# Moving three weight loads, a bias table and three matrix products from the gather loop to behind its last gather

## The chip, the cores and the metric

The kernel runs on one core of one Trainium2 chip. The metric is device time in microseconds (us), the median of three runs. Everything is float32 (the feed-forward part works with products of split numbers).

## What is computed

Two transformer blocks over 256 tokens of 1024 features, batch 1. The change touches the seam between them: the last step of the first block (a layer that picks 128 experts for every token) and the first projections of the second block.

```python
def peer(h, w_pq, sub_keys, u_emb, v_emb):          # end of the first block
    ...                                             # 8 heads, top 16 of 128 x 128 keys each
    def chunk(args):
        hx, idx, g = args                           # idx: 128 experts of each of 128 tokens
        a = jax.nn.gelu(jnp.einsum("ced,cd->ce", u_emb[idx], hx), approximate=False)
        return jnp.einsum("ce,ced->cd", g * a, v_emb[idx])
...
x = x + peer(h2, ...); x = rmsnorm(x, final_g)
...
h = _rmsnorm(x, norm_mix[0])                        # start of the second block, layer 0
p = h @ ev_w_in[0]
qa, ka, va = three slices of p, 512 columns each
c_q, c_kv  = the next 768 and 256 columns of p      # called cqkv below: 1024 columns, two chunks
a_out = _dilated_mixture(qa, ka, va, t5_bias)       # attention with a bias table over distances
b_out = _mla(c_q, c_kv, ...)
```

## The kernel before, in words

The 256 tokens are two tiles of 128 (t = 0, 1), one token per partition. Each engine runs its own list of instructions in the order in which it is written, with semaphores between them.

**The gather loop.** For each tile there are 128 rows of experts (8 heads times 16, `SLOTS`), 256 in all. Row n is one indirect transfer (GpSimd, L568) that brings for each of the 128 tokens the 1024 numbers of u and the 1024 of v of one expert, 1 MB in all, into one of 8 buffers (`NROWS`, tile name `gath`, which the profile shows as `pool`). VectorE multiplies the u half with the token and sums it (L1566, `dot`), ScalarE makes the weight of the row, two rows at a time (L1143, L1147), and a diagonal matrix of it (L1153), TensorE multiplies the v half with the diagonal and adds it up in PSUM (L850). Then the buffer is spent (`row_spent`), and the gather of row n + 8 may be issued: `wait_spent` before L568. VectorE also selects the experts of later heads between its dots, and TensorE makes the scores for that (`query`, L611 and L825) in the first tile at every eighth row, up to row 39.

**Weights** come as one stream of chunks of up to 2 MB through a ring of three slots (`ring`), issued by SyncE at L532 in one fixed list, each when the last use of the chunk three before it is through. The chunks of this case are `va` (one) and `cqkv` (two), which follow the four chunks of the queries, `pq`; then `qa`, `ka`, `kpe_uq`. So `va` is loaded when the product `("pq", 3)` is done, and `cqkv` 0 and 1 after `("pq", 5)` and `("pq", 7)`, the last of which stands at rows 15 and 31 of tile 0.

**The bias table** `tab` (1.5 MB, `t_scratch` in the profile) is issued by GpSimd at L574, right after the gather of row 128, since its place is taken by the keys of the queries until then. VectorE waits for it before the attention `attA`.

**The second block in the shadow of the first.** When tile 0 is complete, its final norm and the next norm are made at rows 2 to 10 of the next tile, the transposes at row 15 (`NORM_SLOT`), and TensorE makes tile 0's products of `va`, `cqkv` 0 and `cqkv` 1 (`token_chunk`, 8 multiplications of 128x512 each, L611) at rows 31, 55 and 79 (`TOKEN_SLOTS`) of tile 1. ScalarE copies each out of PSUM (`token_copy`, L942) 8 rows later (`TOKEN_LAG`).

**Behind the last row**, the same is done for tile 1: VectorE adds the sums (L1576), ScalarE and VectorE make the two norms (L946, L947, L1334, L1341), VectorE clears `kaz` (L481, L482), TensorE transposes (L644), VectorE applies the gain (L1348), TensorE makes the three products of tile 1 (L611), then in split form the products `qa` and `ka` (L716 to L718), whose weights ScalarE and VectorE split into two parts (L1003, L1328), and then the attention `attA` begins (L674). PSUM has six banks for all of this, taken in turn in the order of one list, `fill_list`.

Of the kernel before, what the change touches and what calls it, by code (L numbers as in the profile page):

```python
# [22 lines left out]
P = 128  # L23
S = 256
NT = S // P
# [5 lines left out]
PH, TOPK, NKEYS = 8, 16, 128  # L31
SLOTS = PH * TOPK
# [3 lines left out]
HEADS2 = 8  # L36
# [90 lines left out]
EARLY_QUERIES = 7  # L127
TOKEN_CHUNKS = (("va", 0), ("cqkv", 0), ("cqkv", 1))
NORM_SLOT = 15
TOKEN_SLOTS = (31, 55, 79)  # L130
TOKEN_LAG = 8
QUERY_EVERY = 8


def fill_list():
    out = [("t5",)] + norm_fills("N1") + fm_fills("glu", 4) + tm_fills("q1", 2) + tm_fills("kv1")
    out += fm_fills("gate", 4)
    out += [("q1T", t, half) for t in range(NT) for half in range(2)] + [("k1T",), ("mean",), ("var",)]
    out += attention_fills("att1", QH)
    out += fm_fills("convout", 2) + fm_fills("attno", 2) + tm_fills("wout", 2)  # L140
    out += norm_fills("N2")
    out += QUERY_ORDER
    for t in range(NT):
        out += [("mix0", t, half) for half in range(2)] + [(name, i, t) for name, i in TOKEN_CHUNKS]
    out += fm_fills("qa") + fm_fills("ka")
    out += attention_fills("attA", HEADS2)
    out += norm_fills("cT") + tm_fills("kpe") + tm_fills("uqa") + tm_fills("uqb") + tm_fills("ukv", 2)
    out += [(n, t, half) for n in ("qmT", "kmT") for t in range(NT) for half in range(2)]
    out += attention_fills("attB", HEADS2) + tm_fills("evout", 2)
    for layer in range(2):  # L150
        if layer:
            out += norm_fills("mix1") + tm_fills("uz") + tm_fills("vz") + fm_fills("qd") + fm_fills("kd")
            out += tm_fills("vd") + [("gating", t) for t in range(NT)] + [("coutT", t) for t in range(NT)]
            out += attention_fills("attD", HEADS2) + tm_fills("odout", 2)
        out += norm_fills("ffn%d" % layer) + fm_fills("gu%d" % layer, KF // 2)
        out += [("down%d" % layer, half, t) for half in range(2) for t in range(NT)]
    return out
# [47 lines left out]
def last_use(chunk):  # L205
    return LAST_USE.get(chunk, (chunk[0], chunk[1], 1))
# [10 lines left out]
def build(nc, stream, consts, t5const, params, rows, keys_in, late_rows, x_in, positions, t5_in, rpb_in, uv, out):  # L217
    with ExitStack() as ctx:
# [300 lines left out]
        @block.sync  # L519
        def _(sp):  # L520
            sp.dma_start(x[:, :, :], x_in.rearrange("(t p) d -> p t d", p=P)).then_inc(x_landed, 16)
            sp.dma_start(cst[:, :], consts).then_inc(const_landed, 16)
            sp.dma_start(par[:, :], params).then_inc(param_landed, 16)
            for n, (name, width) in enumerate(CHUNKS):
                if n >= NSLOT:
                    before = CHUNKS[n - NSLOT][0]
                    if before in CHUNK_SPLIT:
                        sp.wait_ge(lo_split, CHUNK_SPLIT[before])
                    else:
                        sp.wait_ge(bank_filled, FILL_NO[last_use(before)] + 1)  # L530
                src = stream[CHUNK_AT[n]:CHUNK_AT[n + 1]].rearrange("(p w) -> p w", p=P)
                sp.dma_start(ring[:, n % NSLOT, 0:width], src).then_inc(chunk_landed[n % NSLOT], 16)  # L532
            for t in range(NT):
                sp.wait_ge(out_ready, t + 1)
                sp.dma_start(out[P * t:P * t + P, :], xn[:, t, :]).then_inc(out_stored, 16)
            sp.wait_ge(out_stored, 16 * NT)


        @block.gpsimd
        def _(gp):  # L540
            gp.dma_start(pos_i[:, :], positions).then_inc(pos_landed, 16)
            gp.dma_start(t5hot, t5const[0:32, :]).then_inc(t5_landed, 16)
            gp.dma_start(t5ln, t5const[32:32 + HEADS2, :]).then_inc(t5_landed, 16)
            gp.dma_start(t5tab, t5_in).then_inc(t5_landed, 16)
            gp.dma_start(row[:, :], rows.to_broadcast([P, NROW])).then_inc(row_landed, 16)
            gp.dma_start(keys.rearrange("p m n -> p (m n)"), keys_in).then_inc(keys_landed, 16)

            nc.gpsimd.memset(rpb_pad, 0.0).then_inc(rpb_cleared, 1)
            gp.wait_ge(rpb_cleared, 1)
            rp = rpb_pad.rearrange("h (r c) -> h r c", r=15)  # L550
            gp.dma_start(rp[:, :, 48:79], rpb_in).then_inc(rpb_landed, 16)
            gp.wait_ge(rpb_landed, 16)
            for r in range(RPB_ROWS):
                gp.dma_start(rpb_dram[:, r], rp[:, r + 4, :].unsqueeze(1).to_broadcast([HEADS2, GRID, P])
                             ).then_inc(rpb_stored, 16)

            wait_emptied(gp, ("t5",))
            gp.dma_start(t5_dram, t5vec.unsqueeze(1).to_broadcast([HEADS2, P, REL])).then_inc(t5_stored, 16)
            gp.wait_ge(t5_stored, 16)
            gp.wait_ge(rpb_stored, 16 * RPB_ROWS)  # L560


            for n in range(NT * SLOTS):
                if n % TOPK == 0:
                    gp.wait_ge(selected, n // TOPK + 1)
                if n >= NROWS:
                    wait_spent(gp, n - NROWS)
                gp.indirect_dma_start(out=gath[:, n % NROWS, :], out_offset=None, in_=uv,  # L568
                                      in_offset=bass.IndirectOffsetOnAxis(ap=experts[:, n:n + 1], axis=0)
                                      ).then_inc(row_landed_in[n % NROWS], 16)  # L570
                if n == SLOTS:

                    gp.wait_ge(bank_filled, FILL_NO[("sc", PH - 1)] + 1)
                    gp.dma_start(tab[:, :, :], bass.AP(tensor=t5_dram.tensor, offset=S - P,  # L574
                                                       ap=[[REL - 1, P], [P * REL, HEADS2], [1, TABW]])
                                 ).then_inc(taba_landed, 16)


            gp.wait_ge(bank_filled, FILL_NO[("attA", "OT", 0, 0)] + 1)
            for qr in range(2):  # L580
                for h in range(HEADS2):

                    gp.dma_start(tab[GRID * qr:GRID * qr + GRID, h, :].rearrange("p (r c) -> p r c", r=6),
                                 bass.AP(tensor=rpb_dram.tensor, offset=(h * RPB_ROWS + 1 - qr) * GRID * P + GRID - 1,
                                         ap=[[P - 1, GRID], [GRID * P, 6], [1, GRID]])).then_inc(tabd_landed, 16)
            gp.dma_start(row[:, LATE["final2"][0]:LATE["final2"][1]],
                         late_rows[:, 0:D].to_broadcast([P, D])).then_inc(late_landed, 16)
            gp.dma_start(row[:, LATE["v_gain"][0]:LATE["v_gain"][1]],
                         late_rows[:, D:D + CW].to_broadcast([P, CW])).then_inc(late_landed, 16)
            gp.wait_ge(tabd_landed, 16 * 2 * HEADS2)  # L590
            blocks = tab[:, :, :].rearrange("p h (r c) -> p (h r) c", c=GRID)
            nc.gpsimd.tensor_tensor(blocks, blocks, c_("namask").unsqueeze(1).to_broadcast([P, 6 * HEADS2, GRID]),
                                    ALU.add).then_inc(tabd_ready, 1)
# [3 lines left out]
        def _(pe):  # L597
# [234 lines left out]
            for t in range(NT):  # L832
                if t:
                    pe.wait_ge(sums_added, 2 * t)
                for k in range(SLOTS):
# [4 lines left out]
                        queries += 2  # L840
                    if t and k == NORM_SLOT:
                        tile_transposes("mix0", 0, xn[:, 0, :])
                    if t and k in TOKEN_SLOTS:
                        if k == TOKEN_SLOTS[0]:
                            wait_tile("mix0", 0)
                        name, i = TOKEN_CHUNKS[TOKEN_SLOTS.index(k)]
                        token_chunk(name, i, 0)
                    pe.wait_ge(diag_ready, n + 1)
                    for half in range(2):
                        last = nc.tensor.matmul(psum[:, RB + half, :], diag[:, n % NDIAG, :],  # L850
# [4 lines left out]
                    if k < SLOTS - 1:  # L855
                        last.then_inc(row_spent, 1)

            tile_transposes("mix0", 1, xn[:, 1, :])
            wait_tile("mix0", 1)
            for name, i in TOKEN_CHUNKS:  # L860
                token_chunk(name, i, 1)
            pe.wait_ge(h_split, 4)
            for q in range(FIRST_PART[0], GU):
                split_feature_major(0, q, (m_hi, m_lo))
# [65 lines left out]
        def _(act):  # L930
# [206 lines left out]
            for pair in range(NT * SLOTS // 2):  # L1137
# [26 lines left out]
                if unit == PH and k == 4:  # L1164
                    act.wait_ge(x_normed, 1)
                    root(x[:, 0, :], xn[:, 0, :], ssq[:, 0:1], 0, D)
                slot = 2 * (pair - SLOTS // 2) + 1 - TOKEN_LAG
                if slot in TOKEN_SLOTS:
                    token_copy(TOKEN_SLOTS.index(slot), 0)

            act.wait_ge(sums_added, 2 * NT)
            root(x[:, 1, :], xn[:, 1, :], ssq[:, 1:2], 1, D)
            act.wait_ge(x_normed, NT)
            root(x[:, 1, :], xn[:, 1, :], ssq[:, 1:2], 1, D)
            token_copy(0, 1)
            split_high(0, 6)
            token_copy(1, 1)
            split_high(0, 7)
            token_copy(2, 1)
            for t in range(NT):  # L1180
# [621 lines left out]
```

## Time and profile before

| | |
|---|---|
| median of 3 runs | 1775.72 us (1775.6 to 1777.1) |
| the profiled execution | 1774.15 us |
| its span, first to last instruction | 1772.1 us |
| granted TensorE clock, mean | 0.953 |
| gathers, first issued to last landed | about 359 to 1036 us |
| TensorE busy | 1515.9 us (86%) |
| VectorE, ScalarE, GpSimd busy | 959.1, 561.8, 315.6 us |
| bytes moved by DMA | 428.67 MB, mean 242 GB/s |
| gathers (queue q0, nearly all) | 279.20 MB |
| weights (queue q1) | 148.33 MB |

How to read it: the busy shares are averages over stages with different limits. TensorE leads in sum, but in the 677 us of gathers the DMA engines are the busiest resource, and on both sides of them TensorE is. What an instruction costs is therefore read from its own stage: from the chain of waits there, and from the DMA rate beside it.

### The profile page before, as it was taken

Reading aid. Unit: us, or ns where it says so; the run is one execution under the profiler, and the core shown is the slowest. Engines: PE = TensorE matmul, PEld = TensorE weight load, DVE = VectorE, ACT = ScalarE, POOL = GpSimd, SP = SyncE. Lnnn points to the kernel's source line nnn. Section 1 sums busy time; section 2 is a strip of 40 time slices with the busy share of each in tenths; the row PEclk is TensorE's granted clock in tenths of the full one; section 3 lists DMA queues with packets and bytes.
Section 4 is the critical chain, followed back from the end, with each engine's and each line's share of the span. In section 5 each row is a group of like instructions: output and inputs, shape, how many; then the busy total and the mean of one; then the engine's idle time right before and its main releaser. Section 6 shows DMA issues by size and latency. Waiting matters only on the chain.

```text
span 1772.1 us, 18024 instructions
## 1 busy us (share of the span) xinstructions
PE 1515.9 (86%) x6822; PEld 1057.0 (60%) x6822; DVE 959.1 (54%) x1916; ACT 561.8 (32%) x1195; POOL 315.6 (18%) x296
## 2 busy tenths in 40 slices
PE   6999699879987777678988769986999969869997
PEld 5768587555533322233333227664999869559996
DVE  2896431375576677677766443233555454245554
ACT  1001530123333333433333224342333334333333
POOL 2000000033344444344445400400000000000000
PEclk9999899989999999899999989998999979989999
DMA  9964013299999999999999935313344523124551
GB/s 258 201 199 171 4 48 143 95 387 385 395 420 419 420 419 418 394 419 410 410 419 415 420 141 223 102 48 142 146 187 190 194 102 147 68 108 180 190 190 48
DMA packets 52022, 428.67 MB, mean 242 GB/s; under 512 B 6880, under 2 KB 7032, under 8 KB 9824
## 3 DMA queue, kind: packets, MB, share of 16 engines
q0 software_dynamic: 40720, 279.20, 40.8%
q1 hardware_dynamic: 11216, 148.33, 22.0%
q8 instruction: 54, 0.88, 0.2%
q14 instruction: 32, 0.26, 0.0%
HBM read 422.50 MB, written 4.98 MB: 241 GB/s over the span
## 4 chain that ended last, share of the span: by engine, by line
PE 66%; DMA 17%; DVE 9%; ACT 5%; issue 2%; POOL 1%; DVEq 0%; SPq 0%; ACTq 0%; POOLq 0%
PE psum L611 24%; DMA pool<-uv,experts 16%; PE psum L850 11%; PE psum L716 9%; PE psum L717 9%; PE psum L718 9%; DVE pool L1566 2%; PE psum L644 2%; PE psum L674 2%; DMA ring<-stream 1%; DVE w_lo L1328 1%; ACT xn L946 1%; ACT diag L1153 1%; POOL pool L568 1%; ACT L1143 1%
## 5 line engine op out<-in xcount | busy, mean ns | idle before, releaser
L850 PE MATMUL psum<-pool,diag 128*128 128x512 f32 x1024 | 487.7, 627 | 132.0 <-ACT diag L1153 122.0
L850 PEld LDWEIGHTS psum<-pool,diag 128*128 128x128 f32 x1024 | 196.1, 199 | 418.1 <-issue 210.9
L1566 DVE CUSTOM_DVE_ANT_0 pool<-pool,xn 128x1024 f32<-128x1024 f32 x256 | 313.8, 1226 | 207.5 <-DMA pool<-uv,experts 205.9
L568 POOL DMA_INDIRECT pool<-uv,experts x256 | 283.7, 1108 | 703.9 <-PE psum L850 359.0
L1328 DVE TENSOR_TENSOR w_lo<-ring,w_hi 128x2048 fp32r<-128x2048 f32 x76 | 173.9, 2292 | 182.7 <-ACT w_hi L1003 182.7
L1003 ACT ACTIVATE w_hi<-ring 128x2048 fp32r<-128x2048 f32 x76 | 145.0, 1911 | 284.7 <-PE psum L718 284.7
L716 PE MATMUL psum<-h_hi,w_hi 128*128 128x256 f32 x704 | 201.4, 286 | 22.4 <-DVE h_lo L1367 22.4
L717 PE MATMUL psum<-h_lo,w_hi 128*128 128x256 f32 x704 | 201.0, 286 | 0.0
L718 PE MATMUL psum<-h_hi,w_lo 128*128 128x256 f32 x704 | 200.9, 285 | 0.0
L611 PE MATMUL psum<-hT,ring 128*128 128x256 f32 x768 | 171.1, 385 | 5.5 <-DMA ring<-stream 2.9
L611 PEld LDWEIGHTS psum<-hT,ring 128*128 128x128 f32 x768 | 148.1, 193 | 28.8 <-issue 5.1
L716 PEld LDWEIGHTS psum<-h_hi,w_hi 128*128 128x128 f32 x704 | 137.1, 195 | 22.8 <-issue 22.8
L717 PEld LDWEIGHTS psum<-h_lo,w_hi 128*128 128x128 f32 x704 | 137.2, 195 | 0.0
L718 PEld LDWEIGHTS psum<-h_hi,w_lo 128*128 128x128 f32 x704 | 137.0, 195 | 0.0
L1143 ACT ACTIVATE acts<-dots 128x2 f32<-128x2 f32 x128 | 25.9, 202 | 333.9 <-DVE dots L1566 333.8
L611 PE MATMUL psum<-ring,hT 128*128 128x512 f32 (+2 forms) x288 | 111.5, 547 | 6.4 <-DVE hT L1502 3.2
L1439 DVE SCALAR_TENSOR_TENSOR pool<-pool,par 128x256 f32<-128x256 f32 x236 | 93.8, 489 | 0.0
L1153 ACT ACTIVATE diag<-cst,coef 128x128 f32<-128x128 f32 x256 | 89.7, 394 | 12.2 <-PE psum L850 8.1
L611 PEld LDWEIGHTS psum<-ring,hT 128*128 128x128 f32 x288 | 53.6, 195 | 62.9 <-issue 56.2
L942 ACT ACTIVATE att<-psum 128x512 f32<-128x512 f32 x69 | 40.5, 588 | 92.4 <-PE psum L611 69.4
L716 PE MATMUL psum<-w_hi,gu_hi 128*128 128x512 f32 x176 | 68.5, 389 | 0.0
L717 PE MATMUL psum<-w_lo,gu_hi 128*128 128x512 f32 x176 | 68.5, 389 | 0.0
(234 smaller groups left out, 1774.3 us busy)
## 6 DMA issues: line engine op xcount, KB each, us to landing
ring<-stream SPq DMA_DIRECT2D x66, 2048.0 KB, 7.9
pool<-uv,experts POOLq DMA_INDIRECT x256, 12.5
ring<-stream SPq DMA_DIRECT2D x3, 1024.0 KB, 6.0
t_scratch<-att POOLq DMA_DIRECT2D x1, 2048.0 KB, 90.8
rpb_scratch<-att POOLq DMA_DIRECT2D x7, 256.0 KB, 28.2
ring<-stream SPq DMA_DIRECT2D x1, 1792.0 KB, 10.2
row<-rows POOLq DMA_DIRECT2D x1, 1672.0 KB, 15.4
ring<-stream SPq DMA_DIRECT2D x1, 1664.0 KB, 7.0
```

The source lines that it names most:

```text
L568: gp.indirect_dma_start(out=gath[:, n % NROWS, :], out_offset=None, in_=uv, in_offset=bass.IndirectOffsetOnAxis(ap=experts[:, n:n + 1], ax ...
L611: last = nc.tensor.matmul(dst, lhsT, rhs, start=(i == 0), stop=(i == len(pairs) - 1))
L716: nc.tensor.matmul(dst, lhsT[0], rhs[0], start=start, stop=False)
L717: nc.tensor.matmul(dst, lhsT[0], rhs[1], start=False, stop=False)
L718: return nc.tensor.matmul(dst, lhsT[1], rhs[0], start=False, stop=stop)
L850: last = nc.tensor.matmul(psum[:, RB + half, :], diag[:, n % NDIAG, :], gath[:, n % NROWS, D + 512 * half:D + 512 * half + 512], start=k = ...
L1003: nc.scalar.activation(part_split(split_tensors(layer, q)[0], layer, q), part_raw(layer, q), ACT.Copy).then_inc(hi_split, 1)
L1143: nc.scalar.activation(acts[:, b, :], dots[:, b, :], ACT.Gelu).then_inc(acts_ready, 1)
L1153: nc.scalar.activation(diag[:, n % NDIAG, :], ident, ACT.Copy, scale=coef[:, b, j:j + 1]).then_inc(diag_ready, 1)
L1328: V.tensor_tensor(lo, part_raw(layer, q), hi.bitcast(F32), ALU.subtract).then_inc(lo_split, 1)
L1439: n = mark(V.scalar_tensor_tensor(y[:, m, :], src, tap, y[:, m, :], ALU.mult, ALU.add))
L1566: ins = V.tensor_tensor_reduce(out=row_u, in0=row_u, in1=xn[:, n // SLOTS, :], scale=1.0, scalar=0.0, op0=ALU.mult, op1=ALU.add, accum_out ...
```

## The change

- SyncE waits before the chunk `va` until row 247 of 256 is spent. That is what the last gather waits for too, so `va` and, right behind it, `cqkv` 0 and 1 are issued together with the last gather.
- GpSimd issues `tab` behind the last gather instead of behind that of row 128.
- TensorE no longer makes tile 0's three products at rows 31, 55 and 79. Behind the last row it makes `va` of tile 0, the transposes of tile 1, `va` of tile 1, and then `cqkv` 0 of both tiles and `cqkv` 1 of both.
- ScalarE's copies of tile 0's products move behind the norms of tile 1, between the others.
- The list of PSUM banks follows the new order.

```diff
@@ fill_list
-    for t in range(NT):
-        out += [("mix0", t, half) for half in range(2)] + [(name, i, t) for name, i in TOKEN_CHUNKS]
+    out += [("mix0", 0, 0), ("mix0", 0, 1), ("va", 0, 0), ("mix0", 1, 0), ("mix0", 1, 1), ("va", 0, 1)]
+    out += [("cqkv", i, t) for i in range(2) for t in range(NT)]
@@ SyncE, before the load of a chunk
+                if (name, width) == (("va", 0), 4096):
+                    wait_spent(sp, NT * SLOTS - NROWS - 1)
                 src = stream[CHUNK_AT[n]:CHUNK_AT[n + 1]].rearrange("(p w) -> p w", p=P)
@@ GpSimd
-                if n == SLOTS:
-
-                    gp.wait_ge(bank_filled, FILL_NO[("sc", PH - 1)] + 1)
-                    gp.dma_start(tab[:, :, :], bass.AP(...)).then_inc(taba_landed, 16)
+            gp.wait_ge(bank_filled, FILL_NO[("mix0", 0, 0)] + 1)
+            gp.dma_start(tab[:, :, :], bass.AP(...)).then_inc(taba_landed, 16)
@@ TensorE
-                    if t and k in TOKEN_SLOTS:
-                        if k == TOKEN_SLOTS[0]:
-                            wait_tile("mix0", 0)
-                        name, i = TOKEN_CHUNKS[TOKEN_SLOTS.index(k)]
-                        token_chunk(name, i, 0)
...
+            wait_tile("mix0", 0)
+            token_chunk("va", 0, 0)
             tile_transposes("mix0", 1, xn[:, 1, :])
             wait_tile("mix0", 1)
-            for name, i in TOKEN_CHUNKS:
-                token_chunk(name, i, 1)
+            token_chunk("va", 0, 1)
+            for i in range(2):
+                for t in range(NT):
+                    token_chunk("cqkv", i, t)
@@ ScalarE
-                slot = 2 * (pair - SLOTS // 2) + 1 - TOKEN_LAG
-                if slot in TOKEN_SLOTS:
-                    token_copy(TOKEN_SLOTS.index(slot), 0)
...
+            token_copy(0, 0)
             token_copy(0, 1)
+            token_copy(1, 0)
             split_high(0, 6)
             token_copy(1, 1)
+            token_copy(2, 0)
             split_high(0, 7)
             token_copy(2, 1)
```

TensorE's order from the second tile on, before. L850 are the products of the rows (two for each row), L644 the transposes of `mix0`, L611 with `ring,hT` the products of `va` and `cqkv`, eight each:

```order
81 L850 MATMUL psum<-pool,diag 128x512 x208
82 L644 MATMUL psum<-cst,xn 128x128 x8
83 L850 MATMUL psum<-pool,diag 128x512 x32
84 L611 MATMUL psum<-ring,hT 128x512 x8
85 L850 MATMUL psum<-pool,diag 128x512 x48
86 L611 MATMUL psum<-ring,hT 128x512 x8
87 L850 MATMUL psum<-pool,diag 128x512 x48
88 L611 MATMUL psum<-ring,hT 128x512 x8
89 L850 MATMUL psum<-pool,diag 128x512 x98
90 L644 MATMUL psum<-cst,xn 128x128 x8
91 L611 MATMUL psum<-ring,hT 128x512 x24
```

and with the change, where L850, L644 and L611 have become L843, L642 and L609:

```order
81 L843 MATMUL psum<-pool,diag 128x512 x208
82 L642 MATMUL psum<-cst,xn 128x128 x8
83 L843 MATMUL psum<-pool,diag 128x512 x226
84 L609 MATMUL psum<-ring,hT 128x512 x8
85 L642 MATMUL psum<-cst,xn 128x128 x8
86 L609 MATMUL psum<-ring,hT 128x512 x40
```

The 24 products that stood between the rows are gone from there; 8 of them stand ahead of the last transposes and 16 among the 40 behind.

SyncE's queue with the change; the rows ahead of the new wait are the chunks up to the last of `pq`:

```order
6 L532 DMA ring<-stream 128x2048 [waits bank_filled]
7 L532 DMA ring<-stream 128x4096 [waits bank_filled] x14
8 L532 DMA ring<-stream 128x4096 [waits row_spent,bank_filled]
9 L532 DMA ring<-stream 128x4096 [waits bank_filled] x4
10 L532 DMA ring<-stream 128x3328 [waits bank_filled]
```

Row 8 there is `va`, which waits for the rows of the gather loop too; behind it stand `cqkv` 0 and 1, `qa` and `ka`, which keep their own waits.

## Rows read from the trace of the kernel before

**Rows 1.** The page, 40 slices of 44.3 us: rate that the DMA moved.

```profile
GB/s 258 201 199 171 4 48 143 95 387 385 395 420 419 420 419 418 394 419 410 410 419 415 420 141 223 102 48 142 146 187 190 194 102 147 68 108 180 190 190 48
```

**Rows 2.** Chain of waits, early gathers: start us, us, what.

```profile
380.19 14.55 PE psum L850 x28
...
477.28 13.80 PE psum L850 x28
...
496.73 11.47 DMA pool<-uv,experts
```

**Rows 3.** Stretches, early gathers: us, PE, PEld, DVE, ACT, POOL busy, PEclk, DMA share, GB/s.

```profile
476.00:480.00 4.00, 2.72 (x3) 1.17 (x4) 2.92 (x11) 3.28 (x14) 0.00 (x0) 0.62 0.98 414
480.00:484.00 4.00, 4.00 (x10) 1.86 (x9) 0.63 (x2) 0.80 (x2) 1.87 (x2) 0.95 0.94 344
484.00:488.00 4.00, 4.00 (x11) 1.80 (x10) 2.17 (x7) 1.38 (x5) 1.88 (x2) 1.00 0.97 330
```

**Rows 4.** DMA queues 475 to 481 us; chunk issued 471.75 us, size, us to landing.

```profile
q1 hardware_dynamic: 125, 2.02, 79.2%
q0 software_dynamic: 80, 0.52, 20.9%
...
ring<-stream SPq DMA_DIRECT2D x1, 2048.0 KB, 12.1
```

**Rows 5.** Chain of waits at the switch to tile 1.

```profile
702.36 16.66 DMA pool<-uv,experts
...
755.11 12.60 DMA pool<-uv,experts
```

**Rows 6.** Who waited for whom, whole run: us in total, times, longest.

```profile
PE psum L850 <- DVE x L1576: 9.8, 1, 9.8
```

**Rows 7.** Stretches in tile 1; the first, third, fourth hold one product each.

```profile
796.00:812.00 16.00, 15.90 (x37) 7.14 (x38) 12.86 (x38) 7.37 (x20) 5.31 (x5) 1.00 0.98 393
812.00:856.00 44.00, 36.41 (x76) 14.75 (x74) 31.31 (x80) 14.52 (x46) 22.21 (x19) 0.92 1.01 421
856.00:872.00 16.00, 15.51 (x37) 6.76 (x36) 9.93 (x21) 5.13 (x19) 5.38 (x6) 1.00 0.99 398
...
917.00:933.00 16.00, 15.19 (x36) 6.82 (x37) 12.18 (x36) 8.02 (x22) 5.91 (x6) 1.00 1.00 403
```

**Rows 8.** Last gather: its issue, us to landing, queue 1022 to 1036 us, its dot.

```profile
1022.51 0.94 POOL L568 DMA_INDIRECT pool<-uv,experts  x1 [0.78 <-PE psum L850]
...
pool<-uv,experts POOLq DMA_INDIRECT x1, 13.5
...
q0 software_dynamic: 691, 4.98, 85.7%
...
1036.00 1.23 DVE L1566 CUSTOM_DVE_ANT_0 pool<-pool,xn 128x1024 f32<-128x1024 f32 x1 [1.13 <-DMA pool<-uv,experts]
```

**Rows 9.** Timeline behind the last row: start us, us, instruction, [idle before it, releaser].

```profile
1049.75 1.97 PE L644 MATMUL psum<-cst,xn 128*128 128x128 f32 x8 [7.58 <-DVE xn L1341]
...
1051.96 1.29 DVE L1348 TENSOR_TENSOR hT<-psum,par 128x512 f32<-128x512 f32 x2
...
1053.35 22.76 PE L611 MATMUL psum<-ring,hT 128*128 128x512 f32 x48 [1.63 <-DVE hT L1348]
```

**Rows 10.** Chain of waits: one product of tile 0 (16 records).

```profile
798.09 6.87 PE psum L611 x16
```

**Rows 11.** Stretches behind the gathers.

```profile
1052.00:1054.00 2.00, 0.65 (x1) 0.50 (x2) 1.97 (x4) 0.00 (x0) 0.00 (x0) 0.50 0.00 0
...
1058.00:1060.00 2.00, 2.00 (x6) 0.87 (x5) 0.00 (x0) 0.00 (x0) 0.00 (x0) 1.00 0.00 0
...
1076.00:1099.00 23.00, 23.00 (x193) 22.93 (x191) 7.93 (x11) 10.22 (x19) 0.00 (x0) 1.00 0.64 249
```

**Rows 12.** Timeline: split of qa's weights; first use of the bias table.

```profile
1070.59 1.91 ACT L1003 ACTIVATE mw_hi<-ring 128x2048 fp32r<-128x2048 f32 x1 [7.59 <-DMA ring<-stream]
...
1101.88 0.76 DVE L1298 SCALAR_TENSOR_TENSOR att<-psum,tab 128x256 f32<-128x256 f32 x2 [7.55 <-PE psum L674]
```

More of the change, by code:

```diff
@@ L129 @@
 NORM_SLOT = 15
-TOKEN_SLOTS = (31, 55, 79)
-TOKEN_LAG = 8
 QUERY_EVERY = 8
@@ L570, in _ @@
                                       ).then_inc(row_landed_in[n % NROWS], 16)
-                if n == SLOTS:
-                    gp.wait_ge(bank_filled, FILL_NO[("sc", PH - 1)] + 1)
-                    gp.dma_start(tab[:, :, :], bass.AP(tensor=t5_dram.tensor, offset=S - P,
-                                                       ap=[[REL - 1, P], [P * REL, HEADS2], [1, TABW]])
-                                 ).then_inc(taba_landed, 16)
+            gp.wait_ge(bank_filled, FILL_NO[("mix0", 0, 0)] + 1)
+            gp.dma_start(tab[:, :, :], bass.AP(tensor=t5_dram.tensor, offset=S - P,
+                                               ap=[[REL - 1, P], [P * REL, HEADS2], [1, TABW]])
+                         ).then_inc(taba_landed, 16)
             gp.wait_ge(bank_filled, FILL_NO[("attA", "OT", 0, 0)] + 1)
```

## The prediction, made before the changed kernel ran

> **What bounds the kernel now.** I read the page's slices first, then the chain of waits, then the DMA rate in short stretches, and the timeline behind the gathers last. From the ninth slice to the 23rd the DMA moves 385 to 420 GB/s [rows 1], and 420 is what it reaches at best there. So the gathers are close to a stage that is bound by bytes, and a first sum would say: 6.29 MB of weights (three chunks of 2048 KB) and 1.57 MB of table (1536 KB) leave it, which at 420 GB/s is 15.0 and 3.7 us. The chain of waits says that this is only partly so. From 380 to 496 us it is TensorE, whose rows and query products follow each other (28 records of row products in 14.55 us, and so on), with no gather in it [rows 2]; the first piece in it that is a gather begins at 496.73. All three chunks are loaded before that (the last is issued at 471.75 [rows 4]). From 497 us to the last gather the chain runs through gathers, one after the other. Behind the last row first the norms and then TensorE are the bound: it computes without a gap from 1053.35 to 1099 us [rows 9, 11].
>
> **The chunks, where they leave.** A chunk hurts the gathers if the DMA would have been busy with them at that time. The last of the three, issued at 471.75 us, is the clearest [rows 4]: while it runs the DMA is full (414 GB/s), but in the 8 us right behind it the rate falls to 344 and 330 [rows 3]. A DMA that slackens there has caught up: nearly all gathers that may be issued have landed, and the next waits for TensorE to spend a row. TensorE is busy throughout those 8 us. So the chunk filled time that TensorE's pace left free. The other two are loaded earlier in the same stretch of the chain, where TensorE's pieces are whole [rows 2]. I take the gain as 0. The other bound is the whole 15.0 us of their bytes; a loss isn't to be had from taking a load away. I stay at 0 since the slack rows lie exactly behind the chunk.
>
> **The table, where it leaves.** It is issued at the switch to tile 1, in the stretch that the gathers do bound. The gather behind it stands 16.66 us in the chain, the next such piece 12.60 [rows 5]: 4.1 us, and the bytes alone make 3.7. What follows is the addition of tile 0's sums, for which TensorE waits 9.8 us [rows 6], so all of it can come out. Gain 4.1 us, bounds 3.0 and 4.1. At its new place it lands behind the last gather, by my sum near 1057 us of the old clock even with all that is below; the first to read it is VectorE at 1101.88 [rows 12], 45 us of cover.
>
> **The products of tile 0, where they leave.** Each takes TensorE 6.87 us in the middle of the rows [rows 10]. Their stretches of 16 us move 393, 398 and 403 GB/s, where a stretch of 44 us between them moves 421 [rows 7]. Against 420 that is 27, 22 and 17 GB/s for 16 us each, 1.06 MB or 2.5 us. The rest of their 20.6 us is hidden by transfers today. Gain 2.5 us, bounds 0 and 4. ScalarE's three copies leave too, beside an engine that waits for the dots; I put them at nothing.
>
> **The chunks, where they arrive.** This is the first of two costs. SyncE now waits for the row that the last gather waits for too, so all three chunks go out with it. What queues behind that wait on SyncE is only `cqkv` and `qa`, and `qa` waits for a product behind the gathers anyway. But at that moment some gathers are still under way: the last is issued at 1022.51, takes 13.5 us to land, and 4.98 MB move in between [rows 8]. The question is who is served first. The row to ask is the time in which chunk and gathers ran together, 475 to 481 us: q1, the weights, moved 2.02 MB, q0, the gathers, 0.52 [rows 4]. At 79% of the 423 GB/s that both make up three chunks take 18.7 us, while the gathers move 1.7 MB; the last gather lands when all is through, (4.98 + 6.29) MB / 420 = 26.8 us instead of 11.9. So the end of the gathers is late by the full 6.29 MB, 15.0 us, and TensorE, which makes the last sum 6 us after that, has nothing to do meanwhile: `va` of tile 0, though landed, stands behind the last row in its order. Cost 15.0 us. The lower bound is a fair share by bytes: as much weight as gather until the last gather is in, 4.98 / 0.42 = 11.9 us. Gathers first would be 0, which the row speaks against by four to one.
>
> The Trainium skill ("DMA: Bandwidth & Descriptors", section "Queues, rings and completion order") says that each DMA engine goes round robin between the queues it has work for, a packet at a time. Taken as equal bytes for both it would give the 11.9 us and not 15.0; the trace's 2.02 against 0.52 MB doesn't agree with that reading.
>
> **The products, where they arrive.** The second cost. `va` of tile 0 comes first and falls into the 7.58 us in which TensorE waits for the norm [rows 9]: 6.87 us fit, and VectorE's clearing of `kaz` holds the next step to 1051.96 in any case. If it fits worse, by a cold clock, up to 2 us. Behind the transposes stand 5 products instead of 3. The three take 22.76 us, of which the first records run at a granted clock of 0.50 and the later ones at 1.00 [rows 9, 11]. With TensorE at work in the gap I expect the full clock from the start: 5 x 6.87 = 34.4 us, so +11.6; with the same slow start it would be +13.7. All of it is on the path, since TensorE is without a gap until the attention. ScalarE and VectorE keep up: `qa` is still loaded after `va` of tile 1, 8 us later it is split [rows 12], long before TensorE comes to it, and `ka` is loaded two products before its turn. The banks repeat after six, and the first reuse (`cqkv` 1 of tile 0 over `va` of tile 0) is five products later.
>
> **The sum**, against the profiled execution: -0 - 4.1 - 2.5 + 15.0 + 11.6 = +20.0 us, 1774.15 to 1794.2. The median of the runs is 1.6 above that execution, so 1795.7.
>
> **Rivals.**
> - *A fair share.* Chunks and gathers move equal bytes: 11.9 for 15.0, 1792.6. For it: two queues on the same engines. Against it: [rows 4]. 0.14.
> - *The bytes counted after all.* Without the chunks the early gathers run ahead and hand on some of the 15.0 us: half of it gives 1788.2, all of it 1780.7. For it: 385 to 395 GB/s in slices that are nearly full [rows 1]. Against it: the chain. 0.10.
> - *Gathers first.* The indirect transfers, being queued already, are served and the chunks fill what is left: no 15.0 us, and 1780.7. `va` would land 5 us behind the last gather, still before its product. 0.05.
> - *Faster.* The weights leave a byte-bound stage (-15.0) and, served last, come back for nothing: -15.0 - 4.1 - 2.5 + 11.6 = -10.0, 1765.7. It turns when gain less delay of the chunks passes 5.0 us, as 11.6 of products stand against 6.6 of the rest. It needs both of the two above. 0.03.
> - *A cold clock.* With one gather in about 12 us for some 19 us TensorE idles, and the last two pairs of rows and the first product run at half clock, as at 1052 us [rows 11]: 3.7 us for a pair turns into 7.4, and `va` outlasts its gap. Up to 6 us more, 1801.7. Against it: the clock is back at 1.00 within 4 to 6 us of work there [rows 11]. 0.13.
> - *The change isn't what it says*: some wait keeps the chunks back until behind the last row. Then no 15.0 us, but TensorE waits some 10 us for `va`, near 1790. I find none. 0.02.
>
> **How the numbers follow.** The forecast as such has 0.52, the cases beside it 0.14, 0.10, 0.05, 0.03, 0.13 and 0.02. The range 1783 to 1802 takes in the fair share, half or less of the bytes, and most of the cold clock, with 0.85 of the chance by these cases. A measurement of this kernel can't tell 0.2% (3.6 us) from no change. Faster by more than that: 0.03. Within: 0.02, where the faster case gets only part of its gain. Slower: 0.95.
>
> **What would show it.** In the profile of the changed kernel: the last gather issued near 1016 us, 6.6 earlier, and 28 us or so to its landing instead of 13.5; in between q1 with four times the bytes of q0; the last dot near 1044. The rate near 480 us still below 420 with no weights in it, which would confirm the 0; if the chain of waits reaches its first gather well before 496 and the last gather is issued before 1013, the 0 was wrong. Rates near 420 through rows 31, 55 and 79 of tile 1. `va` of tile 0 within the norms, then 80 records of products in 34 to 36 us, and the attention's first scores near 1120 instead of 1100. I would be wrong above all if the last gather takes less than 20 us to land.

## The result, and the profile after

| | before | changed |
|---|---|---|
| median | 1775.66 us (1769.5 to 1777.1, 4 runs) | 1801.3 us (1799.4 to 1801.8, 4 runs) |
| profiled execution | 1774.15 | 1801.6 |
| its span | 1772.1 | 1799.5 |
| mean granted clock | 0.953 | 0.955 |

The ratio is 1.0149, 95% interval 1.0124 to 1.0174. The kernel is slower by 25.6 us where +20.0 was forecast. One execution among those of the experiments below (of the products alone) took 6936 us, and is left out of every ratio.

The chain of waits of the changed kernel (start us, us, what; the lines have moved by two to seven, so L843 is the old L850, L609 the old L611, L1563 the old L1566), from the loop's last rows on:

```profile
997.75 13.48 DMA pool<-uv,experts
...
1013.73 3.71 PE psum L843 x8
...
1017.70 28.20 DMA pool<-uv,experts
...
1045.93 1.23 DVE pool L1563
...
1048.40 6.38 PE psum L843 x8
...
1065.93 34.57 PE psum L609 x80
...
1125.07 1.11 PE psum L672 x4
...
1151.89 29.43 PE psum L609 x92
```

The gather in the chain before the last takes 13.48 us, the last one 28.20, where [rows 8] have 13.5. The pair of rows behind it takes 6.38 us and not 3.71. Then come 80 records of products in 34.57 us, for 48 in 22.76 [rows 9]. The DMA queues between 1019.5 and 1038 us (packets, MB, share of 16 engines) tell who moved. Here q1 carries the weights and q0 the gathers:

```profile
q1 hardware_dynamic: 336, 4.98, 63.5%
q0 software_dynamic: 407, 2.90, 37.5%
```

The stretches of that time show what TensorE had of it (us, PE, PEld, DVE, ACT, POOL busy, granted clock, DMA share, GB/s):

```profile
1028.00:1032.00 4.00, 0.00 (x0) 0.00 (x0) 1.23 (x2) 0.00 (x0) 0.00 (x0) 0.74 1.05 444
1032.00:1036.00 4.00, 0.00 (x0) 0.00 (x0) 0.01 (x1) 0.00 (x0) 0.00 (x0) 0.50 1.03 433
1036.00:1040.00 4.00, 1.54 (x2) 0.84 (x3) 1.23 (x2) 1.38 (x5) 0.00 (x0) 0.50 0.98 407
1040.00:1044.00 4.00, 4.00 (x6) 1.52 (x5) 0.45 (x1) 0.00 (x0) 0.00 (x0) 0.56 0.97 382
```

The DMA is full and every engine waits for it; the clock stands at 0.50 when rows come again.

Against the spans of both profiled executions the account is as follows. Each time is a start in a timeline or chain of waits of either kernel.

| stretch | before | changed | difference | forecast |
|---|---|---|---|---|
| start to the last gather's issue | 1022.51 | 1017.70 | -4.8 | -6.6 |
| issue to the last dot | 13.49 | 28.23 | +14.7 | +15.0 |
| last dot to attA's first scores | 64.67 | 79.14 | +14.5 | +11.6 |
| first scores to the end of the span | 671.4 | 674.4 | +3.0 | 0 |
| sum | | | +27.4 | +20.0 |

In the third line are 11.8 us of products and 2.7 us of the last pair of rows. The fourth line holds no work that the change touches.

### The profile page after: what moved, and what is told of

Its sections match the earlier page's. It is cut to its first block, busy times and chain, and to the rows that moved or that the text cites. A ratio compares the mean times of both kernels' runs of the same rounds, so it can differ in the third digit from the quotient of the medians.

```text
span 1799.5 us, 18025 instructions
## 1 busy us (share of the span) xinstructions
PE 1518.7 (84%) x6822; PEld 1056.7 (59%) x6822; DVE 958.6 (53%) x1916; ACT 561.8 (31%) x1195; POOL 308.1 (17%) x296
## 4 chain that ended last, share of the span: by engine, by line
PE 62%; DMA 20%; DVE 10%; ACT 5%; issue 3%; POOL 0%; DVEq 0%; SPq 0%; ACTq 0%; POOLq 0%
PE psum L609 23%; DMA pool<-uv,experts 19%; PE psum L843 10%; PE psum L714 8%; PE psum L715 8%; PE psum L716 8%; DVE pool L1563 3%; PE psum L642 2%; PE psum L672 2%; DMA ring<-stream 1%; DVE w_lo L1325 1%; ACT diag L1150 1%; ACT xn L943 1%; ACT L1140 1%; ACT att L968 1%
## 5 line engine op out<-in xcount | busy, mean ns | idle before, releaser
L843 PE MATMUL psum<-pool,diag 128*128 128x512 f32 x1024 | 490.7, 628 | 161.6 <-ACT diag L1150 156.0
L843 PEld LDWEIGHTS psum<-pool,diag 128*128 128x128 f32 x1024 | 194.9, 199 | 452.5 <-ACT diag L1150 239.5
L1563 DVE CUSTOM_DVE_ANT_0 pool<-pool,xn 128x1024 f32<-128x1024 f32 x256 | 313.4, 1226 | 218.3 <-DMA pool<-uv,experts 214.4
L568 POOL DMA_INDIRECT pool<-uv,experts x256 | 276.3, 1079 | 707.3 <-PE psum L843 367.0
L609 PE MATMUL psum<-hT,ring 128*128 128x256 f32 x768 | 171.2, 385 | 5.5 <-DMA ring<-stream 2.9
L609 PEld LDWEIGHTS psum<-hT,ring 128*128 128x128 f32 x768 | 148.1, 193 | 28.8 <-issue 5.1
L609 PE MATMUL psum<-ring,hT 128*128 128x512 f32 (+2 forms) x288 | 110.3, 545 | 8.0 <-DVE hT L1499 3.2
L609 PEld LDWEIGHTS psum<-ring,hT 128*128 128x128 f32 x288 | 54.5, 202 | 62.6 <-issue 54.0
## 6 DMA issues: line engine op xcount, KB each, us to landing
rpb_scratch<-att POOLq DMA_DIRECT2D x7, 256.0 KB, 28.2
```

Of the source, the lines that this page charges most:

```text
L609: last = nc.tensor.matmul(dst, lhsT, rhs, start=(i == 0), stop=(i == len(pairs) - 1))
L1563: ins = V.tensor_tensor_reduce(out=row_u, in0=row_u, in1=xn[:, n // SLOTS, :], scale=1.0, scalar=0.0, op0=ALU.mult, op1=ALU.add, accum_out ...
```

## The experiments

### The early loads of the chunks: what were they worth?

The changed kernel alone says much. In the stretches around the place where the last chunk used to be loaded, it has no weights to move:

```profile
476.00:480.00 4.00, 2.72 (x3) 1.17 (x4) 3.86 (x11) 3.29 (x14) 0.00 (x0) 0.62 0.81 274
480.00:484.00 4.00, 4.00 (x10) 1.85 (x9) 1.71 (x6) 0.96 (x3) 2.17 (x2) 0.96 0.38 84
484.00:488.00 4.00, 4.00 (x11) 1.80 (x10) 1.88 (x5) 1.33 (x5) 2.49 (x3) 1.00 1.02 416
```

Where the kernel before moved 414, 344 and 330 GB/s [rows 3], this one moves 274, 84 and 416: for some 4 us it has next to nothing to do, and TensorE's busy time is the same. The first gather in the chain starts at 496.72 us, as before at 496.73 [rows 2]. To take nothing else away, the kernel before ran with these loads cut down to 32 of 4096 columns, so that the products compute with what stands in the ring:

```diff
+                if name in TOKEN_CHUNKS:
+                    src, width = src[:, 0:32], 32
                 sp.dma_start(ring[:, n % NSLOT, 0:width], src).then_inc(chunk_landed[n % NSLOT], 16)
```

> The kernel before, with the early loads of the three chunks cut to 32 of 4096 columns, so 6.2 MB less are moved; the products of va and cqkv use what stands in the ring, and the result is not the reference's. My theory (the early loads lie in time that TensorE's pace leaves free): 0, at most -1 us. Rival (bytes bound the whole gather loop): -15 us, 1761.

Measured: 1777.42 us against 1777.1, ratio 1.0004 (0.9991 to 1.0017). So with 6.2 MB less nothing is gained in the time, or 1.6 us at most by the interval. Its chain of waits has the same pieces:

```profile
375.39 14.57 PE psum L852 x28
...
472.50 13.81 PE psum L852 x28
...
491.95 10.70 DMA pool<-uv,experts
```

It runs 4.8 us ahead of the kernel before, but its first gather was issued that much earlier already (354.46 against 359.26 us): from the first to the 49th gather both take 137.5 us. From there to the last gather's issue it is 524.8 us against 525.8, so up to 1 us of gain may hide in the scatter.

### The table alone

```diff
-                if n == SLOTS:
-                    gp.wait_ge(bank_filled, FILL_NO[("sc", PH - 1)] + 1)
-                    gp.dma_start(tab[:, :, :], ...)
+            gp.wait_ge(bank_filled, FILL_NO[("mix0", 0, 0)] + 1)
+            gp.dma_start(tab[:, :, :], ...)
```

> Only the bias table moves behind the last gather; weights and products stay where they were. My theory: 4.1 us of the gathers' time come out at the switch to tile 1 and nothing is paid, so -4 to -5 us against the kernel before, about 1771. Rival (the next wait takes it up, since the buffers are full there anyway): within 1 us of before.

Measured: 1772.78 against 1777.1 us, ratio 0.9973 (0.9962 to 0.9984). A second measurement:

> The table alone behind the last gather, in more rounds, beside the version with the moved third product. My theory: ratio 0.996 to 0.998.

Measured: 1773.77 against 1776.46, ratio 0.999 (0.9981 to 1.000), 2.7 us by the medians and 1.8 by the ratio, which is less than was expected. The first gave 4.3 and 4.8. From the 49th gather's issue to the last it takes 522.6 and 522.9 us in the two profiles, against 525.8 before. I take the gain as 3.0 us, at the lower bound of the forecast's term and not the 4.1 taken; the executions alone leave room for 0 to 7 us.

### Products and table, but the chunks early

This is the changed kernel without these two lines:

```diff
-                if (name, width) == (("va", 0), 4096):
-                    wait_spent(sp, NT * SLOTS - NROWS - 1)
```

> The change without SyncE's new wait: the chunks are loaded early as before, table and products of tile 0 stand behind the gathers. My theory: +11.6 for the products, -4.8 for what the loop gains (as the changed kernel's last gather shows), so about +7, 1783; the last gather lands 13.5 us after its issue and not 28. Rival (the weights' early loads did cost the gathers something): the early loads come back, the last gather is issued later than in the changed kernel by up to 15 us, and this kernel is as slow as it, 1800.

Measured: 1785.39 against 1777.1 us, ratio 1.0038 (1.0025 to 1.0051). The chain of waits has both halves of the theory, the last gather at its old length and the 80 records:

```profile
1019.44 13.55 DMA pool<-uv,experts
...
1035.48 3.71 PE psum L841 x8
...
1050.36 36.13 PE psum L607 x80
```

The rival is out as to its size: with the early loads back the last gather isn't issued 15 us later but 1.7 (1019.44 against 1017.70), or 1.9 counted from the 49th gather (522.9 us against 521.0). The loads are all that differs up to there, so these 1.9 us are what the early loads cost, if they aren't scatter. The wait that SyncE got costs 15.9 us by the medians (1801.3 and 1785.4) and 19.7 by the ratios, so it costs far more than it buys.

### The products alone

> Only the products of tile 0 (and ScalarE's copies) move behind the gathers; chunks and table are loaded as before. My theory: +11.6 to +13.4 behind the gathers (five products where three were), -1 in the loop, so +11 to +12 against before. Rival (the products did cost the loop the 2.5 us or more of the forecast): +9 or less.

Measured: 1791.8 us against 1776.24 (1792.1 with the execution of 6936 us), ratio 1.0091 (1.0074 to 1.0108), above what was expected. The profile was of that execution and can't be used. A second measurement:

> The kernel in which only the products of tile 0 move, once more, since its first profile was of a disturbed execution. Its times lay 15.9 us above before (1792.1), where with the table moved too the same edit cost 12.6 (1785.4 against 1772.8 with the table alone). My theory: about 13.4 behind the gathers, and the rest is the scatter of a few us between executions, so +12 to +14 now. Rival (the table at its old place costs more when the products are gone from the loop, or the loop is slower without them): +16 again, and the last gather is issued 2 us or more later, counted from the first gather, than the 663.3 of before.

Measured: 1789.53 against 1776.46, +13.1, ratio 1.0076 (1.0057 to 1.0095). The products behind take 36.27 us (+13.5), and from the 49th to the last gather it is 525.3 us against 525.8. The loop got 0.4 us out of losing three products of 6.87 us each. The table at its old place doesn't cost more when they are gone: +13.1 lies within what was expected, and from the first to the last gather's issue it is 662.8 us, where 663.3 and 2 more would have spoken for that rival.

### The chunks after the last gather

The changed kernel, with another wait for the first chunk:

```diff
                 if (name, width) == (("va", 0), 4096):
-                    wait_spent(sp, NT * SLOTS - NROWS - 1)
+                    sp.wait_ge(row_landed_in[NROWS - 1], 16 * NT * SLOTS // NROWS)
```

> The changed kernel, but SyncE waits until the last gather has landed before it loads the three chunks. My theory (chunks and gathers share the DMA and the gathers lose): the last gather is back to 13.5 us, the last row is through 15 us earlier, the last pair of rows runs at the full clock (-2.7), and the first chunk is there about 8 us after the last landing, so its product still lies mostly in the gap before the norm: 15 to 18 us faster than the changed kernel, 1784 to 1786. Rival (the loss comes from TensorE's products alone and the DMA would have waited in any order): no more than 5 us faster than the changed kernel.

Measured: 1783.25 us against 1777.1, ratio 1.0034 (1.0023 to 1.0044), 18 us less than the changed kernel. Its timeline and chain:

```profile
1017.10 13.55 DMA pool<-uv,experts
1030.72 8.92 DMA ring<-stream
1039.89 8.65 PE psum L609 x16
...
1050.41 34.57 PE psum L609 x80
```

Only 13.6 us later do the same bytes start, the gather is back at 13.55 us, and TensorE waits 3 us for the first chunk. To load the weights *later* brings the last landing 15 us forward. This is the plainest proof that the delay of the last gather comes from what ran beside it.

### One chunk beside the last gathers, not three

```diff
                 if (name, width) == (("va", 0), 4096):
                     wait_spent(sp, NT * SLOTS - NROWS - 1)
+                if (name, width) == (("cqkv", 0), 4096):
+                    sp.wait_ge(row_landed_in[NROWS - 1], 16 * NT * SLOTS // NROWS)
```

> The changed kernel, but only the chunk va goes out with the last gather; cqkv 0 and 1 wait until that gather has landed. My theory (each chunk beside the last gathers delays them by its full bytes, 5.0 us): the last gather takes 18.5 us from issue to landing, and the time is 4 to 5 us above that of the kernel in which all three wait (1783 on the chip of that run), 10 to 11 above before. Rival (a fair share by bytes): one chunk ends before the last gather either way, so the landing can't tell it, but the queue's bytes in the first 6 us do: two of weights for two of gathers, against 2.0 to 0.5 by my theory.

Measured: 1787.53 against 1776.24 us, ratio 1.0063 (1.0046 to 1.008); 0.29% or 5 us above the kernel in which all three wait (1.0034), each against the kernel before that ran beside it. The last gather and its dot, in the timeline:

```profile
1018.17 0.94 POOL L570 DMA_INDIRECT pool<-uv,experts  x1 [0.78 <-PE psum L845]
...
1036.61 1.23 DVE L1565 CUSTOM_DVE_ANT_0 pool<-pool,xn 128x1024 f32<-128x1024 f32 x1 [1.17 <-DMA pool<-uv,experts]
```

From issue to dot it is 18.4 us. The chain of waits goes another way here, through a gather two before it (issued at 1013.18, 18.37 us), as each of the last four gathers is held up alike (17.6 or 18.4 us to landing). So 13.5, 18.4 and 28.2 us for none, one and three chunks: 4.9 us for each, close to 2.1 MB at 420 GB/s.

The shares of the two queues can be read where both have work. First this kernel, 1021 to 1027 us, then the changed one, 1021 to 1042 us, which is all the time that its three chunks move:

```profile
q1 hardware_dynamic: 108, 1.77, 69.8%
q0 software_dynamic: 120, 0.85, 33.9%
...
q1 hardware_dynamic: 412, 6.21, 70.1%
q0 software_dynamic: 406, 2.67, 30.5%
```

That is 2.1 and 2.3 to one, neither the one to one of the rival nor the four to one of the forecast and the expectation. In packets it is 108 to 120 and 412 to 406: both queues get through nearly as many packets, and a packet of weights is more than twice as large (15.1 KB against 6.6 in the changed kernel). The four to one came from [rows 4], and there the queue of the gathers had little to move. In the kernel before GpSimd waited for spent buffers:

```profile
474.60 0.94 POOL L568 DMA_INDIRECT pool<-uv,experts  x1 [8.18 <-PE psum L850]
481.05 0.93 POOL L568 DMA_INDIRECT pool<-uv,experts  x1 [5.52 <-PE psum L850]
```

Only one gather was issued between 466 and 481 us, and from 476 to 479 us q0 moved 0.14 MB beside 1.10 of q1. At two to one, too, the chunks are through before the last gather (1042 against 1046 us), and so their full bytes count.

### The changed kernel once more

> The changed kernel once more, beside the others on one chip. My theory: ratio to before 1.013 to 1.016 as in its first measurement, and in a second profile the same 28 us from issue to landing of the last gather and over 5.5 us for the last pair of rows; of the 3.0 us that its first profile lost behind the first scores of attA, part or all is chance of the clock and changes. Rival (that loss belongs to the change): it stays at 3 us, attA's first scores to the end taking 674 us again against 671.4 before.

Measured: 1800.49 against 1776.24 us, ratio 1.0131 (1.0109 to 1.0153). Its chain repeats the two marks:

```profile
1015.94 28.19 DMA pool<-uv,experts
...
1046.62 6.32 PE psum L843 x8
```

The last pair takes 6.3 to 6.4 us in both profiles of this kernel, and 3.70 or 3.71 us in those of all kernels here whose last gather takes 13.5 us. So the 2.7 us go with the idle time before it: TensorE stands idle for 11.06 us, makes the pair before the last in 6.2 us, is idle for 3.72 and makes the last one in 6.4, at a granted clock of 0.50 (1036 to 1040 and 1048 to 1051 us). The loss behind attA's first scores came again too, against what was expected: 674.5 us from there to the end, and the 92 records of products behind that attention took 29.43 us. But that stretch has three lengths, whatever the kernel: 26.15 us in the kernel before, in both profiles of the table alone, with one chunk and in one of the two profiles of the version below, 27.76 with the late chunks, and 29.4 to 29.5 in the changed kernel (twice), the products alone, products with table, the other profile of the version below, and the kernel with the cut loads, which differs in nothing there from the one before. What differs is how long the clock stands at 0.50 within it: the kernel before had 4 us at 0.57, the changed one, whose three rows follow, about three times as long:

```profile
1132.00:1136.00 4.00, 4.00 (x8) 1.70 (x8) 0.00 (x0) 0.20 (x1) 4.00 (x8) 0.57 0.65 152
...
1152.00:1156.00 4.00, 4.00 (x24) 4.00 (x24) 0.00 (x0) 0.20 (x1) 4.00 (x7) 0.60 0.62 152
1156.00:1160.00 4.00, 4.00 (x13) 2.97 (x14) 0.00 (x0) 0.20 (x1) 3.86 (x7) 0.50 0.62 151
1160.00:1164.00 4.00, 4.00 (x7) 1.52 (x7) 0.00 (x0) 0.00 (x0) 2.89 (x1) 0.62 0.59 200
```

It isn't a matter of the work in that stretch. Of the six profiles of kernels with all of tile 0's products behind the gathers four have 29.4 us, of the six others two; that the change makes it likelier can't be excluded and was not settled. But the whole way from the first scores to the end scatters more than that: 674.7 and 669.3 us in the two profiles of the table alone, 675.3 with the cut loads, 671.4 in the one profile of the kernel before, 674.4 and 674.5 in the changed kernel. The 3.0 us lie within this scatter.

### A version that beats both

The table goes behind the last gather, and of tile 0's products only the third leaves the loop, for the 7.6 us in which TensorE waits for tile 1's norm:

```diff
-TOKEN_SLOTS = (31, 55, 79)
+TOKEN_SLOTS = (31, 55)
@@ TensorE, behind the last row
+            token_chunk("cqkv", 1, 0)
             tile_transposes("mix0", 1, xn[:, 1, :])
@@ ScalarE, behind the norms of tile 1
+            token_copy(2, 0)
             token_copy(0, 1)
```

> A version meant to beat both: the kernel before with the table behind the last gather, and of tile 0's products only the third (cqkv 1) moved, into the 7.5 us in which TensorE waits for the norm of tile 1. My theory: -3.5 for the table, as in the kernel with the table alone, and -2 since the clock stays up and the three products behind take 20.6 to 21 us and not 22.8: -5 to -6 against before, about 2 below the kernel with the table alone. Rival (the product pushes the transposes of tile 1 back, or the clock falls at another place): no faster than the table alone, -4.

Measured: 1769.46 against 1776.24 us, ratio 0.9955 (0.9937 to 0.9973). But its profile didn't bear out the reason for the 2 us: the three products behind took 22.53 us, as the clock fell to 0.50 right behind the 2.5 us that TensorE stands idle after the transposes (0.89 at 1048 to 1050 us, 0.50 at 1050 to 1052). A second measurement:

> Table behind the last gather and tile 0's third product in the gap before tile 1's norm. Its first profile showed the three products behind still at 22.5 us, as the clock fell in the 2.5 us behind the transposes. My theory now: what it gains over the table alone is the third product's share of the loop, 1 us or less; ratio 0.996 to 0.997. Rival (the moved product is worth 2 us or more): 0.995 or less.

Measured: 1770.72 against 1776.46 us, ratio 0.9971 (0.9959 to 0.9982), 3.0 us under the table alone (1773.77), where 1 us or less was expected. In this profile the clock held:

```profile
1016.00 13.51 DMA pool<-uv,experts
...
1032.01 3.71 PE psum L848 x8
...
1046.89 20.84 PE psum L609 x48
```

20.84 us, where two profiles of the table alone show 22.60 and 22.45. One profile in two has the gain of the clock, and from the 49th gather to the last both are shorter than the table alone (521.8 and 521.1 us against 522.6 and 522.9). The version is 5 to 8 us faster than the kernel before, and some 30 faster than the changed one.

## Why the prediction was right or wrong, point by point

- **The chunks where they leave, 0.** Right in the main. The slack right behind the chunk [rows 3] was the right place to look. The idle DMA of the changed kernel and the cut loads confirm it, and the rival in which half or all of the bytes count is out. But the profiles leave a gain of 1.0 us (cut loads) to 1.6 to 1.9 us: from the 49th to the last gather it takes 522.9 us in products with table, and 521.0, 521.1, 521.3 and 521.2 us in the changed kernel (twice), with late chunks and with one chunk, which differ up to there in the early loads alone. The times of the cut loads (ratio 1.0004, 0.9991 to 1.0017) can't resolve that, and two profiles of one kernel differ by up to 0.8 us there.
- **The chunks where they arrive, +15.0.** Right in size (14.7) and cause; none, one and three chunks give it in steps of 4.9 us. The share of four to one was misread from a time in which the queue of the gathers had little to move; with work in both it is 2.1 to 2.3 to one. It doesn't enter the sum. A fair share would have given 25.4 us to the landing; it was 28.2. Gathers first is out.
- **The products where they arrive, +11.6.** Right for this kernel: 34.57 us for 80 records as forecast, in both profiles. The reason given, that `va` of tile 0 keeps TensorE at work, isn't enough. In three other kernels (products alone, products with table, one chunk) `va` fills the same gap and the same 2.50 us of idling follow the transposes, yet the 80 records took 36.1 to 36.3 us, nearer to the upper value of that term. The clock had fallen there; first products with table, then the changed kernel, both where the 80 records begin:

```profile
1050.00:1052.00 2.00, 1.64 (x2) 0.84 (x3) 1.93 (x5) 0.00 (x0) 0.00 (x0) 0.52 0.00 0
...
1066.00:1068.00 2.00, 2.00 (x5) 0.96 (x6) 1.88 (x4) 0.00 (x0) 0.00 (x0) 1.00 0.00 0
```

  Why it held in one and fell in the others is open.
- **The products where they leave, -2.5.** Too much. This is the first step that failed. It took the low rates around rows 31, 55 and 79 [rows 7] as time lost to the last gather. In the changed kernel the same stretches have

```profile
796.00:812.00 16.00, 12.76 (x26) 5.56 (x27) 12.81 (x35) 6.45 (x21) 6.69 (x7) 0.89 1.01 420
856.00:872.00 16.00, 11.10 (x24) 4.31 (x24) 9.13 (x22) 5.13 (x20) 7.25 (x7) 1.00 1.01 419
917.00:933.00 16.00, 12.31 (x25) 5.10 (x25) 12.45 (x36) 6.60 (x21) 5.84 (x7) 0.89 1.00 408
```

  so most of the low rates are gone, yet the products alone brought 0.4 us, and with the table moved too the stretch from the 49th to the last gather took 522.9 us, against 522.6 and 522.9 for the table alone. So 0 to 0.4, in the bounds of 0 and 4, and not 2.5. Where the bytes that seemed lost were made up was not found.
- **The table where it leaves, -4.1.** Slightly too much: 3.0 in the loop. The step read one piece of the chain against the next (16.66 and 12.60); the changed kernel has at the same switch

```profile
708.40 14.37 DMA pool<-uv,experts
```

  and not 12.6, so part of the 16.66 wasn't the table's. The kernel with only the products moved, where the table stays, has 18.54 there.
- **The cold clock.** Put at 0 in the sum and kept as a rival at 0.13. This is the step that cost most of what the change itself does. The forecast itself had TensorE idle for 15 us and, in [rows 11], the model of what follows, and still took the clock to be back in time. It came true for the last pair (+2.7 of the 3.7 that a pair wholly at half clock was said to cost). `va` of tile 0 took 7.03 us behind it and ended 0.7 us before the norm, so it cost nothing.
- **Behind the attention**, +3.0 in the profiled pair: no step had it. It isn't work of the change, and it is no more than two profiles of one kernel differ by there (674.7 and 669.3 us, the table alone). How much of it the medians hold isn't known.
- **The total.** The sign and the mechanism were right, the size was 5.6 us short, and the measured median lies at the upper edge of the range (1801.3 of 1802); by the ratio it is 1802.1. Between the two profiled executions the gap is 7.4 us: 1.8 of gains counted too high (the products' 2.5 and 1.1 of the table's, less 1.8 or so that the chunks' place gave and the sum had at 0), 2.7 of cold clock and 3.0 of the slow stretch later, less 0.1 in the rest. Between the medians it is 5.6, since the profiled execution of before lay 1.5 us under its median and that of the changed kernel at it. The upper end had room for the cold clock and not for both. That the cold-clock rival named 1801.7 is in part luck, as only 2.7 of its 6 us came and the rest is from terms that it didn't have. (The chances of the forecast and its rivals add up to 0.99.)

## What to carry to other kernels

Before bytes are moved out of a stretch, look at the DMA rate right behind the transfer: if it falls while the gathers of the loop wait for a buffer, the transfer filled time that nobody else wanted. A load that is issued together with the last transfers of a loop delays them by its full bytes, even if it is wanted only later: issue it early, in slack, or when the last of them has landed. And where an edit makes TensorE idle ahead of work on the path (here 11.06 and 3.72 us ahead of the last two pairs of rows), put the half clock for the first of that work into the sum, not into a rival.

## What the runs showed that was not expected

- Two queues on the same DMA engines, both with work, moved nearly equal numbers of packets (412 and 406) and so bytes by the size of the packets: 6.21 MB of weights to 2.67 of gathers. A share read where one queue has little to move (2.02 to 0.52 MB [rows 4]) says nothing about that.
- Low rates of the DMA within the loop, 393 to 403 GB/s over 16 us, cost the loop next to nothing, though its own chain runs through gathers.
- The same 92 products behind the attention took 26.15 or 29.45 us in kernels that are the same there, by how long the granted clock stood at 0.50, and also in the two profiles of one kernel. Differences of 3 us between single profiles of this kernel carry no news.
